# A hybrid decoder step on one core: decode states in three buffers during prompt attention, the mask on TensorE, group factors from four columns, weight loads moved

## What is computed

```python
q_a, c_raw, kr_raw, z_attn, z_ssm, xbc, dt_raw = _in_projection(x, lw)
q_lat, q_rope, ckv, k_rope = _mla_qk(q_a, c_raw, kr_raw, pos, lw)
...
sc = jnp.where(k_pos[None, None, None, :] <= q_pos[None, None, :, None], sc, NEG_BIG)
p = jax.nn.softmax(sc, axis=-1).astype(ckv.dtype)
...
y_diag = jnp.einsum('bcgls,bgjcls,bcsgjp->bclgjp', cb, decay_in, xdt)
y_off = jnp.einsum('bclgn,bcgjpn,bgjcl->bclgjp', cc, states[:, :-1], jnp.exp(a_cum))
...
h = jnp.exp(da_t)[..., None, None] * h + jnp.einsum('bgjp,bgn->bgjpn', x_t * dt_t[..., None], b_t)
return h, jnp.einsum('bgjpn,bgn->bgjp', h, c_t)
...
out = _rmsnorm(gated, lw['ssm_norm'].reshape(SSD_GROUPS, D_SSM // SSD_GROUPS))
...
return x + _rmsnorm(mix @ lw['w_out'], lw['norm_post'])
```

## Time and profile before

| | |
|---|---|
| median of 3 runs | 633.62 us (632.35 to 635.15) |
| the profiled execution | 628.45 us |
| its span, first to last instruction | 626.5 us |
| mean granted clock of TensorE | 0.95 |
| busy share | PE 87%, PEld 73%, DVE 64%, ACT 45%, POOL 25% |
| moved | 104.13 MB, mean 166 GB/s |

### The profile page before, as it was taken

One profiled execution on the slowest core, in us unless ns is written; L12 is line 12 of the kernel. 1 busy time (PEld: TensorE's weight loads), 2 busy tenths in 40 slices (PEclk: granted clock), 3 DMA queues, 4 the chain that ended last, 5 costly groups with the idle time before them and its releaser, 6 DMA issues.

```text
span 626.5 us, 12457 instructions
## 1 busy us (share of the span) xinstructions
PE 547.3 (87%) x4716; PEld 460.3 (73%) x4716; DVE 399.4 (64%) x798; ACT 281.2 (45%) x606; POOL 158.1 (25%) x164
## 2 busy tenths in 40 slices
PE   4999989999999999999975999878895387789992
PEld 4999989998888888888852466545553187689991
DVE  5576986726666667444333655676658979986665
ACT  7324122313566654524240543666576545735320
POOL 3110000000000000000012622667366826750523
PEclk9999999979999999999996899899897789999997
DMA  8241123536888888888554011641630066469541
GB/s 337 78 168 60 52 76 104 193 145 215 272 257 266 274 272 269 266 269 268 179 140 133 1 53 30 109 90 54 220 146 17 4 276 223 134 207 387 198 141 68
DMA packets 55774, 104.13 MB, mean 166 GB/s; under 512 B 7274, under 2 KB 26067, under 8 KB 55459
## 3 DMA queue, kind: packets, MB, share of 16 engines
q1 hardware_dynamic: 55714, 103.34, 51.4%
HBM read 95.68 MB, written 7.73 MB: 165 GB/s over the span
## 4 chain that ended last, share of the span: by engine, by line
PE 62%; DVE 18%; issue 6%; ACT 6%; DMA 4%; POOL 3%; SPq 1%; DVEq 0%; POOLq 0%; ACTq 0%
PE pm L1458 15%; PE pm L1460 12%; PE pm L1459 12%; PE px L1541 4%; DVE prod L1134 3%; PE px L1557 3%; DVE w_lo L844 3%; PE pm L1676 2%; DMA w_raw<-in_w_out 2%; DMA w_uv<-in_w_uv 2%; PE pm L1714 1%; PE px L1723 1%; ACT w_hi L529 1%; PE px L1724 1%; PE px L1667 1%
## 5 line engine op out<-in xcount | busy, mean ns | idle before, releaser
L1458 PE MATMUL pm<-xw_hi,w_lo 128*128 128x260 f32 x544 | 163.6, 301 | 9.1 <-DVE w_lo L958 8.1
L1459 PE MATMUL pm<-xw_lo,w_hi 128*128 128x260 f32 x544 | 155.5, 286 | 0.0
L1460 PE MATMUL pm<-xw_hi,w_hi 128*128 128x260 f32 x544 | 155.3, 286 | 0.0
L1458 PEld LDWEIGHTS pm<-xw_hi,w_lo 128*128 128x128 f32 x544 | 104.3, 192 | 24.4 <-issue 11.9
L529 ACT ACTIVATE w_hi<-w_raw 128x1024 fp32r<-128x1024 f32 (+1 forms) x70 | 72.2, 1036 | 105.4 <-PE pm L1460 81.7
L844 DVE TENSOR_TENSOR w_lo<-w_raw,w_hi 128x1024 fp32r<-128x1024 f32 (+1 forms) x70 | 88.3, 1265 | 28.1 <-ACT w_hi L529 28.1
L1459 PEld LDWEIGHTS pm<-xw_lo,w_hi 128*128 128x128 f32 x544 | 104.4, 192 | 0.2
L1460 PEld LDWEIGHTS pm<-xw_hi,w_hi 128*128 128x128 f32 x544 | 104.3, 192 | 0.0
L1458 PE MATMUL pm<-mix_hi,w_lo 128*128 128x260 f32 x256 | 75.0, 293 | 16.3 <-DVE w_lo L844 10.0
L1460 PE MATMUL pm<-mix_hi,w_hi 128*128 128x260 f32 x256 | 73.7, 288 | 0.0
L1458 PEld LDWEIGHTS pm<-mix_hi,w_lo 128*128 128x128 f32 x256 | 49.6, 194 | 18.6 <-DVE w_lo L844 12.0
(11 more groups left out here) (260 smaller groups left out, 1141.3 us busy)
## 6 DMA issues: line engine op xcount, KB each, us to landing
page<-in_cache SPq DMA_DIRECT2D x128, 288.0 KB, 3.4
w_raw<-in_w_in SPq DMA_DIRECT2D x34, 512.0 KB, 4.9
w_raw<-in_w_out SPq DMA_DIRECT2D x32, 512.0 KB, 6.4
dec<-ac_dram SPq DMA_DIRECT2D x16, 256.0 KB, 10.3
hring<-in_ssm_state SPq DMA_DIRECT2D x8, 512.0 KB, 9.2
o_ssms<-hring SPq DMA_DIRECT2D x8, 512.0 KB, 7.2
w_raw<-in_w_qb SPq DMA_DIRECT2D x6, 384.0 KB, 2.9
xraw<-in_xT SPq DMA_DIRECT2D x4, 520.0 KB, 6.2
```

The lines of the kernel that those rows point to most:

```text
L1458: pe.matmul(out, wl, xh, start=start, stop=False)
L1459: pe.matmul(out, wh, xl, start=False, stop=False)
L1460: return pe.matmul(out, wh, xh, start=False, stop=stop)
```

## The change

- **Decode states.** `hring` becomes three buffers outside the space of the SSD states. Quads 0 and 1 are updated in the round ahead of head 0, 2 and 3 in round 0, and so on by the table `QUADS`; only quad 15, and the dots of 13 to 15, stand behind attention. SP stores a state as soon as it is updated and loads a later one into its buffer (`STORES`, `PREV`), after the store has landed and its dots are done.
- **Mask.** PE adds the mask as a third product (128x128, from rounded copies of the identity and the mask) into each score block; DVE's addition goes.
- **Group factors.** PE sums the squares into four columns (`group_totals`), ACT takes the root of 128x4, DVE its reciprocal, ACT scales four identities with it, PE spreads it over the partitions (`group_spread`), ACT copies it.
- **Weight loads.** Five weight buffers for the output projection, three of them in the space of the SSD states; items 40 to 42 are loaded in round 4, and item 45 ahead of 43 and 44. `w_uv` is loaded as soon as `p_pn` is 29, `w_uk` ahead of the decay rows, and the first five decay rows behind `p_pn` 32.
- **Order.** `y_pair(2 * h)` moves behind `outs(h, 0)` on PE; `decays`, `head` and `masked` stand in other places of the round; `masked(h)` of a round is done a round earlier. New layout of the buffers.

```diff
-SLOT_QUADS = {5: {1: 0, 3: 1}, 6: {1: 2, 3: 3}, 7: {1: 4, 3: 5}}
-ITEM_QUADS = {NIN + 6 * (n // 5) + n % 5: 6 + n for n in range(10)}
 FIRST_NEEDS = {(NIN, 0): 13, (NIN, 6): 14, (NIN, 7): 15, (NIN + 1, 7): 16}
-GROUP_SCALE = {4: (0, 1), 5: (2, 3), 6: (4, 5), 7: (6, 7)}
+GROUP_SCALE = {4: (0, 1), 5: (2, 3), 6: (4, 5, 6), 7: (7,)}
 SSM_HIGH = {5: (0, 1), 6: (2, 3), 7: (4, 5, 6, 7)}
-SSM_LOW = {5: (0, 1), 6: (2, 3), 7: (4, 5), 8: (6, 7)}
+SSM_LOW = {5: (0, 1), 6: (2, 3), 7: (4, 5, 6), 8: (7,)}
+GROUP_AT = {3: 0, 5: 1}
+NDEC = 6
+BUF, NTH, PREV = (0, 1, 0, 1, 2, 0, 1, 2), (1, 1, 2, 2, 1, 3, 3, 2), (None, None, 0, 1, None, 2, 3, 4)
+QUADS = {-1: (0, 1), 0: (2, 3), 1: (4,), 2: (5,), 3: (6,), 4: (7, 8), 5: (9, 10), 6: (11, 12), 7: (13, 14)}
+STORES = {0: 0, 1: 1, 3: 2, 4: 3, 5: 4, 6: 5, 7: 6}
...
-        return i % 2 if i < NIN else (i - NIN + 2) % 4
+        return i % 2 if i < NIN else (i - NIN + 2) % 5
...
+            if PREV[b] is not None:
+                sp.wait_ge(s_hst[BUF[b]], 16 * (NTH[b] - 1))
+                sp.wait_ge(v_dot, 8 * (PREV[b] + 1))
+            elif b == 4:
+                sp.wait_ge(p_y, 8)
+            sp.dma_start(hring[BUF[b]], a["ssm_state"][b]).then_inc(s_hl[BUF[b]], 16)
...
+        for k in range(2):
+            sp.dma_start(w_uv[k], a["w_uv"][k]).then_inc(s_kv[k], 16)
+        sp.wait_ge(p_pn, 2 * NPAGE)
+        load_uk(0)
+        load_uk(1)
+        load_acb(0)
+        load_acb(1)
         sp.wait_ge(p_pv, 2)
         sp.dma_start(stS, a["conv_state"]).then_inc(s_sts, 16)
-        for k in range(2):
-            sp.dma_start(w_uv[k], a["w_uv"][k]).then_inc(s_kv[k], 16)
+        load_dxs()
+        load_acb(2)
+        load_acb(3)
+        load_acb(4)
...
+        sp.wait_ge(a_bct, 1)
+        sp.dma_start(bc_dram, u[1][0:32, 0:P]).then_inc(s_bcd, 16)
+        sp.wait_ge(s_bcd, 16)
+        sp.wait_ge(p_cb, 2)
+        sp.wait_ge(v_cs, 1)
+        sp.wait_ge(g_last, XT)
+        load_acb(5)
+        load_bcs(0)
+        load_bcs(1)
...
+        for s in range(H):
+            if s < 3:
+                load_acb(4 * s + 6)
+                load_acb(4 * s + 7)
+                load_ea(2 * s + 2)
+            if s == 4:
+                load_state(4)
+                load_bcs(4)
+                sp.wait_ge(s_ssm, 16)
+                for i in range(NIN, NIN + 3):
+                    load_item(i)
+            if s in STORES:
+                b = STORES[s]
+                store_state(b)
+                b = PREV.index(b) if b in PREV else None
+                if b is not None:
+                    load_state(b)
+                    load_bcs(b)
+            if s < 2:
+                load_acb(4 * s + 8)
+                load_acb(4 * s + 9)
+            if s < 3:
+                load_ea(2 * s + 3)
+            if s + 4 < H:
+                load_uk(s + 4)
+        load_item(NIN + 5)
+        load_item(NIN + 3)
+        load_item(NIN + 4)
+        load_item(NIN + 6)
+        store_state(NB - 1)
         sp.wait_ge(s_out, 48)
-        load_item(NIN + 2)
-        load_item(NIN + 3)
         sp.dma_start(xres_g, a["xT"][:, 0:7]).then_inc(s_xr, 16)
-        for i in range(NIN + 4, NIN + 18):
+        for i in range(NIN + 7, NIN + 18):
...
+        def group_root(g):
+
+            act.wait_ge(p_gt, g + 1)
+            act.activation(rg, px[:, 3, 4 * g:4 * g + 4], ACT.Sqrt, bias=epsc, scale=1.0 / NORM_WIDTH[3 + g]).then_inc(a_gt, 1)
+
+        def group_diagonal(g):
+
+            act.wait_ge(p_y, 8)
+            act.wait_ge(v_gr, g + 1)
+            if g:
+                act.wait_ge(p_gb, g)
+            for c in range(NCH):
+                act.activation(rdiag[:, P * c:P * c + P], cm[:, M_ID, :], ACT.Copy, scale=rg[:, c:c + 1]).then_inc(a_gd, 1)
+
+        def group_copy(g):
+
+            act.wait_ge(p_gb, g + 1)
+            act.activation((r_pre, sqs)[g][:, 0:NT], pm[:, 0, :], ACT.Copy).then_inc(a_gb, 1)
...
+                if b == 1 and 1 <= s <= 3:
+                    decays(4 * s)
+                if b == 2 and 1 <= s <= 3:
+                    decays(4 * s + 1)
+                if b == 0 and s - 1 in GROUP_AT:
+                    group_diagonal(GROUP_AT[s - 1])
             if s < 0:
+                for n in QUADS[s]:
+                    state_decay(n)
                 continue
+            if s in GROUP_AT:
+                group_root(GROUP_AT[s])
+            if s + 2 < H:
+                copy_k(s + 2)
+            if s - 1 in GROUP_AT:
+                group_copy(GROUP_AT[s - 1])
             if s:
                 mix_high(s - 1)
             if 1 <= s <= 3:
-                exp_ea(2 * s)
                 decays(4 * s + 2)
-            if s + 2 < H:
-                copy_k(s + 2)
+            copy_pt(s, 2)
             if 1 <= s <= 3:
                 decays(4 * s + 3)
-            copy_pt(s, 2)
+                exp_ea(2 * s)
             copy_pt(s, 3)
-            for b in range(4):
-                for n in quads(s + 1, b):
-                    state_decay(n)
+            for t in SSM_HIGH.get(s, ()):
+                ssm_high(t)
+            for n in QUADS[s]:
+                state_decay(n)
+            if 1 <= s <= 3:
+                exp_ea(2 * s + 1)
             if 1 <= s <= 4:
                 gated_square(2 * s - 1)
-            if 1 <= s <= 3:
-                exp_ea(2 * s + 1)
-            if 1 <= s <= 2:
-                decays(4 * s + 4)
-                decays(4 * s + 5)
...
-        def mask_max(h, b):
+        def row_max(h, b):
             n = 4 * h + b
             x = px[:, n % 3, :]
             dve.wait_ge(p_s, n + 1)
-            link(dve.tensor_tensor(x[:, P * b:P * b + P], x[:, P * b:P * b + P], cm[:, M_MQ, :], ALU.add))
             dve.tensor_reduce(nmx[:, 4 * (h % 2) + b:4 * (h % 2) + b + 1], x[:, 0:P * (b + 1)], AX.X, ALU.max,
...
+        for h in range(4):
             head(h)
         dve.wait_ge(p_os, 1)
         dve.tensor_tensor(z[:, 0:H, NT:TT], z[:, 0:H, NT:TT], px[:, 3, 128:192].rearrange("p (h b) -> p h b", h=H), ALU.mult)\
            .then_inc(v_os, 1)
-        dve.wait_ge(a_cvs, 2)
-        dve.wait_ge(a_dx, 1)
-        dve.tensor_tensor(dxs[:, 0], xbc[:, 0:8, NT:TT], dxs[:, 0], ALU.mult).then_inc(v_dx, 1)
         dve.wait_ge(v_os, 1)
 
         for s in range(-1, H):
             h = s + 1
             for b in range(4):
                 if h < H:
-                    mask_max(h, b)
-                if b == 0 and 2 <= s <= 3:
-                    head(4 * s)
-                    head(4 * s + 1)
-                if b == 1 and 1 <= s <= 4:
+                    row_max(h, b)
+                if b == 0 and 1 <= s <= 4:
                     y_pair(2 * s - 1)
-                for n in quads(s, b):
-                    if n:
-                        dots(n - 1)
-                if h < H and b:
-                    inverse_sum(h, b - 1)
+                if h < H and b >= 2:
+                    inverse_sum(h, b - 2)
             if h < H:
+                inverse_sum(h, 2)
                 inverse_sum(h, 3)
             if s < 0:
                 continue
-            if s in (4, 6):
-                inverse(s // 2 + 1, (r_pre, sqs)[s // 2 - 2])
+            if s in GROUP_AT:
+                group_inverse(GROUP_AT[s])
+            if 1 <= s <= 3:
+                head(4 * s)
+                head(4 * s + 1)
             if s:
                 mix_low(s - 1)
+            for n in QUADS[s - 1] if s else QUADS[-1]:
+                dots(n)
             if 1 <= s <= 3:
                 head(4 * s + 2)
                 head(4 * s + 3)
@@ -1238,11 +1285,15 @@
             for t in SSM_LOW.get(s, ()):
                 ssm_low(t)
             gated(s)
-            if s in (5, 6):
-                lo(NIN + s - 5)
+            if 6 <= s:
+                lo(NIN + s - 6)
+        lo(NIN + 2)
         for t in SSM_LOW[8]:
             ssm_low(t)
         mix_low(H - 1)
+        dots(13)
+        dots(14)
+        dots(15)
 
 
         def finish(h, m):
@@ -1256,21 +1307,18 @@
             dve.wait_ge(v_scaled, SHARE * h + m + 1)
             dve.tensor_tensor(x, x, (xres_g[:, m] if m < 7 else xres_u)[:, halves[h]], ALU.add).then_inc(v_fin, 1)
 
-        lo(NIN + 2)
+        lo(NIN + 3)
         for i in range(NIN, len(ITEMS)):
-            if i + 3 < len(ITEMS):
-                lo(i + 3)
+            if i + 4 < len(ITEMS):
+                lo(i + 4)
             _, h, m, kk, _ = ITEMS[i]
-            for n in item_quads(i):
-                dots(n - 1)
-            if i == NIN + NOUT - 4:
...
+        def group_totals(g):
+
+            pe.wait_ge(v_y, (6, 8)[g])
             pe.wait_ge(g_sqg, 3 * g + 3)
-            pe.matmul(out, cm[:, M_ONE, :], gacc, start=True, stop=True).then_inc(p_ring, 1)
+            for c in range(NCH):
+                last = pe.matmul(px[:, 3, 4 * g + c:4 * g + c + 1], gacc[g][:, P * c:P * c + P], cm[:, M_ONE, 0:1], start=True, stop=True)
+            last.then_inc(p_gt, 1)
+
+        def group_spread(g):
+
```

(18 more changed lines are left out.)

302 lines of the change are left out of this document (134 added, 168 removed).

## The result

The changed kernel took 642.79 us (median of 4, 639.39 to 644.8), the kernel before 633.13 us beside it (632.35 to 635.15). The ratio is 1.0143, 95% interval 1.0111 to 1.0174: slower by 1.4%, where I had forecast 3.5% faster.

What follows compares the result with a forecast made beforehand. PE was taken to bound the kernel up to 318.5 us and from 503, but often not in between, with DVE the bound in the last round. Terms -8 +8 -11 -11 = -22 us gave 611.5 us from 633.6, range 601 to 623.

Steps and rivals of the forecast that it cites:

- The join, -8: Stage from 318.5 to 371 us: the wait for `w_uv` goes and the third `values_up` starts 8.1 us earlier; -8 us.
- Rounds 0 to 3, +8: Attention rounds from 375.4 to 445.8 us: added waits and dots outweigh removed mask additions; +8 us, bounds +2 and +16.
- The sign of being wrong that I had named: Rounds 0 to 3 above 86 us, which would point to rival B or D.
- +4: Round 2: ACT's square of pair 2 waits for POOL's sum behind `masked(10)` and `masked(11)`, whose rows come late; +4 us.
- rival B: SP's queue, rounds 0 to 5: decay rows wait for store landings and dots; -10 us, 623 (619 to 630); chance 0.21.
- round 1, +3: Round 1: `y_pair(2)` needs heads 4 and 5 on DVE, and two quads of dots stand ahead of `head(6)`; +3 us.
- Rounds 4 to 7, -11: Rounds from 445.8 to 503 us: 15.7 us removed, 5 of the added work on the path; -11 us, bounds -5 and -15.
- 15.7 us removed: Rounds 4 to 7: two reciprocals of 3.33 us, 12 mask additions (3.5 us) and PE's 5.5 us output-projection wait go.
- Rival D: Port shared by DVE and POOL: 52 moved dots cost 1.30 us each, half the excess on path; +4, 637.6 us; chance 0.04.
- point of decision: Rival D decides from 0.42 us more per dot on the path (22/52).
- The output projection, -11: Last stage, from 503 to 613.3 us: most stalls go as updates leave; 99 us, -11 us, bounds -16 and -6.
- the 4 us that I gave to item 43: Output projection: item 43's load must wait for attention's end and the store of state 6; 4 us.

Runs made afterwards that it cites:

- e2_sum: The changed kernel with POOL's second sum of squares of a round moved ahead of the maskings of the two late decay rows: 632.05 us, ratio 1.0000.
- e3_queue_sum: The changed kernel with that earlier sum on POOL, and decay, ea and w_uk loads ahead of the next state's load on SP's queue: 635.87 us, 1.0041.

## Why the prediction was wrong

**The join, -8: right in kind, 3.5 us kept in this execution.** The wait for `w_uv` went. The term mis-sized is the landing of `stS`: I took 8.8 us, it took 12.7 behind `w_uk` and two decay rows (2.1 with nothing ahead of it):

```profile
stS<-in_conv_state SPq DMA_DIRECT2D x1, 144.0 KB, 12.7
```

It landed at 335.9 us instead of the forecast 331.8; the convolution behind it took 2.3 us instead of the 4.0 that I used, which gave some of that back. The third `values_up` came 5.7 us earlier, not 8.1, and heads 0 and 1 gave back 2.2. The same code up to here began round 0 at 367.9 us in `e2_sum` (`stS` in 10.9 us, 0.45 given back) and at 374.0 in `e3_queue_sum` (`stS` in 12.4 us), 7.5 and 1.4 earlier than before, so the size of this term is not settled.

**Rounds 0 to 3, +8: measured +22.5. Two steps failed.** The sign of being wrong that I had named, rounds 0 to 3 above 86 us, came: 92.9. Round 0 was right (+2.2 for +2). Round 2 has the mechanism that I named, POOL's sum behind `masked(10)` and `masked(11)`, but not at +4: one line moved took 11.1 us off round 2 and 8.2 off the four rounds. The step that failed is this price. I took the wait for a row and nothing behind it: POOL's sum held ACT for 5.60 us, the exponentials behind ACT's square held TensorE for 7.35, and the keys after that took 3.78 us instead of 1.98, a term for the clock that I had left out. The queue, rival B's condition, to which I had given 0.21, has a part in it: 8.4 us in which SP waited for a store stood ahead of these rows. But its order alone gained 3.4 us in rounds 0 to 3, and nothing once the sum stood earlier, so B isn't what decided. The second step is round 1, +3 and measured +5.7: the dots ahead of `head(6)` took 4.35 us instead of 2.3 (399.80 to 404.15), and `y_pair(3)` waited 3.43 us behind them instead of 1.58. Without any dots that wait is 1.60 us again, but round 1 still takes 22.0, so they aren't its whole cause.

What stays open: without the wait for the sum and without any update these rounds take 79.7 us for 70.4. The old place of `y_pair` doesn't win them back (81.8 us), and nothing suggests the mask on TensorE, since VectorE's is 2.7 us longer there; the rest was not isolated. Decay exponentials that now stand between those of the scores, and the clock of 0.88 to 0.90 in rounds 1 to 3 (0.92 to 0.97 before), are in the trace and were not tested apart. The early updates' own 5.2 us (84.9 for 79.7) aren't in the dots.

**Rounds 4 to 7, -11: measured +4.1. Two steps failed here too.** The first is "DVE has dots of seven quads there instead of five, 8 x 0.29 = 2.3 us". Dots took 16.5 us there for 9.5 before, 7.0 more, in bursts of eight ahead of the operations that TensorE waits for, and without them the stage takes 49.2 us. The second is that 15.7 us removed would come off the path but for 5. VectorE did work 5.3 us less than before (40.27 for 45.52), and the stage still grew. Of the terms, the start of the output projection gave 2.5 us of its 5.5 (2.97 for 5.51); the masks gave 0.5 of their 3.5 behind round 3; and the reciprocals, 6.7 us, are free in a kernel with 8 dots in these rounds. What they were worth with 28 dots there no run shows. Since the stage without any dots is only 8.0 us shorter than before, a right price for the dots alone would not have made -11 right: how much of the 15 us of error belongs to each of the two steps stays open.

Rival D had the mechanism and put the chance at 0.04; its price was too high (1.01 us more for each of 52; measured 0.24 more on the mean, 529 ns), and it counted 52 dots as moved, where 20 of them stood in rounds 5 to 7 before the change. Its point of decision was too far, because I spread it over all rounds, while 10.1 of the 12 us that go without dots are in the two waits of rounds 6 and 7. The prediction itself quoted the rule of the Trainium skill, SBUF — State Buffer, section "SBUF: two separate sides", said that by it the move costs more than 0.29 us, and then used 0.29. The trace agrees with the rule: 0.29 us with POOL idle, up to 1.39 beside it.

**The output projection, -11: measured -9.8.** No wait for `w_lo` remained, and 100.5 us compare with my 99. That was right in the main, in part by luck: the 4 us that I gave to item 43 didn't come, and 3.58 us within item 40 went to a late part of `mixlo_s`, which I hadn't counted. One line of that sum is wrong as well: it says that fifteen of sixteen quads leave this stage, but ten were updated in it before and one is now, so nine leave (44 dots before, 12 now). It was dear, too: emptying it of updates moved them to where they cost 12 us, and eight of them fit in it at 0.5 us.

**The sum.** -3.5 +22.5 +4.1 -9.8 for -8 +8 -11 -11. With the sum of squares and eight updates placed otherwise, the change is 1.8% faster than before: 620.3 us, about half of the 22 us that I forecast for the change as it was written. Of the 31 us between my 611.5 and the measured 642.8, two places in the order account for some 22; the other 9 no run here won back.

## What to carry to other kernels

When VectorE's work moves to a stage where POOL is busy, take its duration from a row with POOL at work, multiply it by the length of the burst that stands ahead of an operation that is waited for, and count what already stood there. Work that is removed from an engine counts only if nothing else takes its place in that wait. A wait for late data is to be priced by everything queued behind it on that engine, here a 1.3 us sum whose place cost 8 us of the stage, and cheap orders of one line are to be tried before anything is moved. Work beside a stage that TensorE fills is nearly free until its loads meet the weights on the queue.

## What the runs showed of the hardware

- An idle TensorE can pay twice. In the changed kernel the four products of the keys took 1.98 us after a wait of 0.36 or 1.96 us and 3.78 us after one of 7.35; round 2's mean granted clock was 0.78 with the wait and 0.95 without it. The length of the last wait doesn't decide it alone: in `e2_sum` the same products took 3.68 us after the same 1.96 us of round 1:

```profile
391.81 3.68 PE L1773 MATMUL pm<-ckv,w_uk 128*128 128x512 f32 x4 [1.96 <-ACT pt L770]
```

- VectorE's other operations were held by POOL as well: `COPY u<-z` of 128x8 took 1.22 us beside POOL's `group_scale` and 0.17 us elsewhere, and two `mixlo_s` products 3.48 us instead of 1.41. That is no effect of the change; before it the same two took 1.22 and 3.42 us in round 7:

```profile
512.37 3.48 DVE L1232 SCALAR_TENSOR_TENSOR mixlo_s<-xbc,cols,mix_hi 128x512 fp32r<-128x512 f32 x2
515.78 1.22 DVE L1221 COPY u<-z 128x8 f32<-128x8 f32 x1
```

- The landing of a transfer depends on what was issued before it: 512 KB of `w_uv` took 4.0, 10.8 and 16.9 us, and 144 KB of `stS` 2.1, 8.8 and 12.7 us, in three places of the queue. In one and the same place `stS` took 12.7, 11.2 and 10.9 us in three kernels.
